# Third attention branch of a two-block network: upper turned pieces moved to idle score banks, a head pair's first scores put inside a projection, sum and gate of the output reordered

## What is computed

```python
qc = partial_rope(cq.reshape(B, S, C_HEADS, C_HEAD_DIM), positions)
kc = partial_rope(ck.reshape(B, S, C_HEADS, C_HEAD_DIM), positions)
for window, dil in ((128, 1), (512, 4), (2048, 16)):
    o_p, lse_p = dilated_window_attention(qc, kc, vc, window, dil)
wts = softmax(stack(lses), axis=0)
oc = sum(wts * stack(outs), axis=0)
yc = oc.reshape(B, S, C_WIDTH) * silu(cz)
```

## Time and profile before

| | |
|---|---|
| median of 3 runs | 3854.07 us (3852.71 to 3858.39) |
| the profiled execution | 3863.39 us, span 3861.7 us |
| TensorE busy | 3637.6 us, 94% of the span |
| VectorE, ScalarE, GpSimd busy | 1884.9, 1352.8, 1089.7 us |
| mean granted TensorE clock | 0.968 |

### The profile page before, as it was taken

One profiled execution on the slowest core, in us unless ns is written; L12 is line 12 of the kernel. 1 busy time (PEld: TensorE's weight loads), 2 busy tenths in 40 slices (PEclk: granted clock), 3 DMA queues, 4 the chain that ended last, 5 costly groups with the idle time before them and its releaser, 6 DMA issues.

```text
span 3861.7 us, 49543 instructions
## 1 busy us (share of the span) xinstructions
PE 3637.6 (94%) x19870; PEld 3212.0 (83%) x19870; DVE 1884.9 (49%) x3582; ACT 1352.8 (35%) x2965; POOL 1089.7 (28%) x794
## 2 busy tenths in 40 slices
PE   6999998988898999999999888899999999999998
PEld 5888887877777788888877777778999999999998
DVE  5444555455556364155635554555424546434543
ACT  3112444054443121044422444522225641224541
POOL 3633222311212345323323111223531013531102
PEclk9999999999999999999999999999999999999999
DMA  3121111411113311201122111152110013211012
GB/s 111 39 85 60 34 42 52 147 38 37 36 33 136 126 60 55 82 31 41 44 97 94 43 40 33 44 181 85 59 53 29 24 48 105 69 48 36 25 38 94
DMA packets 85478, 244.83 MB, mean 63 GB/s; under 512 B 10752, under 2 KB 24832, under 8 KB 85248
## 3 DMA queue, kind: packets, MB, share of 16 engines
q1 hardware_dynamic: 85248, 241.66, 18.8%
HBM read 191.09 MB, written 50.53 MB: 63 GB/s over the span
## 4 chain that ended last, share of the span: by engine, by line
PE 74%; DVE 12%; ACT 7%; issue 3%; POOL 2%; DMA 1%; SPq 0%; DVEq 0%; POOLq 0%; ACTq 0%
PE pj L1567 30%; PE pS L1567 26%; PE po L1817 3%; PE pS L1797 3%; PE pS L1799 2%; PE pS L1661 1%; PE pS L1662 1%; DVE tmp L2497 1%; DVE PC L2670 1%; ACT P L2029 1%; DVE tmp L2494 1%; DVE KK L2506 1%; PE po L1683 1%; PE po L1709 1%; ACT P L2022 1%
## 5 line engine op out<-in xcount | busy, mean ns | idle before, releaser
L2988 POOL TENSOR_SCALAR Whi<-stage 128x1024 fp32r<-128x1024 f32 (+3 forms) x252 | 259.6, 1030 | 1945.9 <-PE pj L1567 1241.7
L1567 PE MATMUL pj<-Hhi,Whi 128*128 128x512 f32 x1640 | 671.0, 409 | 51.4 <-DVE PC L2670 40.9
L1567 PE MATMUL pj<-Hlo,Whi 128*128 128x512 f32 x1640 | 654.7, 399 | 0.0
L1567 PE MATMUL pj<-Hhi,Wlo 128*128 128x512 f32 x1640 | 654.5, 399 | 0.0
L2990 POOL TENSOR_TENSOR Wlo<-stage,Whi 128x1024 fp32r<-128x1024 f32 (+3 forms) x252 | 599.5, 2379 | 21.0
L1567 PEld LDWEIGHTS pj<-Hhi,Whi 128*128 128x128 f32 x1640 | 320.3, 195 | 127.8 <-DVE PC L2670 48.8
L1567 PEld LDWEIGHTS pj<-Hhi,Wlo 128*128 128x128 f32 x1640 | 317.1, 193 | 70.2
L1567 PEld LDWEIGHTS pj<-Hlo,Whi 128*128 128x128 f32 x1640 | 318.8, 194 | 62.3
L1567 PE MATMUL pS<-Hhi,Whi 128*128 128x512 f32 x792 | 315.1, 398 | 20.9 <-DVE Hlo L2359 9.9
L1567 PE MATMUL pS<-Hlo,Whi 128*128 128x512 f32 x792 | 312.4, 394 | 0.0
L1567 PE MATMUL pS<-Hhi,Wlo 128*128 128x512 f32 x792 | 312.1, 394 | 0.0
(11 more groups left out here) (484 smaller groups left out, 7973.6 us busy)
## 6 DMA issues: line engine op xcount, KB each, us to landing
stage<-wstream SPq DMA_DIRECT2D x228, 512.0 KB, 3.6
merged<-Mb SPq DMA_DIRECT2D x32, 512.0 KB, 2.9
Mb<-merged SPq DMA_DIRECT2D x32, 512.0 KB, 5.2
gates<-tmp SPq DMA_DIRECT2D x48, 256.0 KB, 2.2
TH<-gates SPq DMA_DIRECT2D x24, 512.0 KB, 6.1
xres<-X SPq DMA_DIRECT2D x16, 520.0 KB, 2.9
xr<-xres SPq DMA_DIRECT2D x16, 520.0 KB, 3.9
X<-xT SPq DMA_DIRECT2D x16, 256.0 KB, 7.0
```

Of the source, the lines that this page charges most:

```text
L1567: x = pe.e.matmul(ps, w[a][:, v.koff + k * P:v.koff + k * P + P], moving(v.of, b, k, v.t0, v.n), start=k == 0 and i == 0, stop=k == v.K - ...
L2988: pool.e.tensor_scalar(upper, stage, 1.0, 0.0, ALU.mult, ALU.add).then_inc(*pool.tick("whi", c))
```

## The change

Three edits, all in the third branch of the first block:

1. In the last query block of a head (`i` = 3), the third and the fourth piece are turned into banks 3 and 5, which that step's own scores have left and the next scores (`i` = 0) don't need. Before, the fourth went to bank 3, and the third took one of the projection banks 0 and 1.
2. The first scores of the next head pair are issued inside the second half of the query projection, behind its fifth slice, instead of behind the whole of it; that projection moves from before `soft(s + 1)` into the list of projections behind it. So VectorE and ScalarE take the softmax of these scores before they rotate that projection.
3. `gather(s - 1)` stands behind the pieces of step `s`, not ahead of them. Its multiplication by the gate moves into `gather_out`, behind `soft(s + 1)`, as one operation on 64x512 for every two steps instead of two on 64x256.

```diff
--- before.py
+++ after.py
@@ -754,10 +754,10 @@
 
         def attended(soft, scores):
             self.banks = WIDE
-            turned = self.bank_free[3]
+            turned = self.bank_free[3], self.bank_free[5]
             self.bank_free[2:6] = [("masked", soft.id, m) for m in (0, 0, 1, 1)]
             if not diff:
-                self.bank_free[3] = turned
+                self.bank_free[3], self.bank_free[5] = turned
             self.mask_free = ("masked", soft.id, 1)
             self.th_free = self.phase()
             self.mb_free = ("scores", scores.id, 1)
@@ -896,11 +896,12 @@
             return dict(l=l, diff=False, s=s, j=j, h=h, qb=2 * i, nb=2 * i + 2, maps=[(h, 2 * i), (h, 2 * i + 1)],
                         col=96 + 12 * (s % 8), p=[0, 1])
 
-        def scores(s):
+        def scores(s, within=False):
             j, h, i = steps[s]
             keys = [qk["q"][i // 2], qk["k"][0]] + ([qk["k"][1]] if i >= 2 else [])
-            scored[s] = self.put("scores", **geometry(s), ready=[x for y in keys for x in y] + [cleared],
+            scored[s] = self.put("scores", **geometry(s), within=within, ready=[x for y in keys for x in y] + [cleared],
                                  free=[("masked", softened[s - 1].id, m) if s else None for m in (0, 0, 1, 1)])
+            return scored[s]
 
         def soft(s):
             softened[s] = self.put("soft_c", **geometry(s), scores=scored[s].id, p_free=p_free[:], masks=("masks_in", 2 * l + 1))
@@ -917,10 +918,10 @@
             u = self.put("turns_c", **geometry(s), **more, parts=parts, soft=softened[s].id,
                          pt_free2=("valued", valued[s - 1].id) if s else None)
             last = ("pt_low", s, l) + parts[-1][0:2]
-            if n == 3:
-
-                u["bank"], u["free"] = 3, ("masked", softened[s].id, 0)
-                self.bank_free[3] = last
+            if n > 1 and steps[s][2] == 3:
+
+                u["bank"], u["free"] = 2 * n - 1, ("masked", softened[s].id, n - 2)
+                self.bank_free[u.bank] = last
             elif n:
                 u["bank"], u["free"] = self.take()
                 self.bank_free[u.bank] = last
@@ -938,8 +939,7 @@
 
         def gather(s):
             j, h, i = steps[s]
-            u = self.put("gather", **geometry(s), i=i, valued=valued[s].id, y_free=self.y_free, z_ready=ztok[i // 2],
-                         tmp_free=self.tmp_free[3])
+            u = self.put("gather", **geometry(s), i=i, valued=valued[s].id, tmp_free=self.tmp_free[3])
             self.po_free = ("gathered", u.id)
             if i % 2:
                 gathered[s] = u
@@ -947,7 +947,7 @@
         def gather_out(s):
             j, h, i = steps[s]
             if s in gathered:
-                u = self.put("gather_out", **geometry(s), i=i, of=gathered[s], y_free=self.y_free)
+                u = self.put("gather_out", **geometry(s), i=i, of=gathered[s], z_ready=ztok[i // 2], y_free=self.y_free)
                 self.tmp_free[3] = ("lo", u.id)
                 if h:
                     self.ytok[i // 2].append(("lo", u.id))
@@ -968,15 +968,17 @@
                     amid[6], amid[7] = [q[0], g[3], k[0]], k[1:2]
                     fresh, turned = v[0:3], v[3:]
             todo = amid[s % 8]
+            for f in range(len(pieces(s))):
+                turn(s, f)
             if s:
                 gather(s - 1)
-            for f in range(len(pieces(s))):
-                turn(s, f)
             if s % 8 == 7 and j < 3:
 
-                self.run(q[1:2])
+                q[1]["inside"] = {4: [scores(s + 1, True)]}
+                todo = q[1:2] + todo
+            elif more:
+                scores(s + 1)
             if more:
-                scores(s + 1)
                 soft(s + 1)
             if s % 8 == 6 and j < 3:
                 read += [("scores", scored[s + 1].id, m) for m in range(2)]
@@ -2070,7 +2072,7 @@
 
     def gather_out(u):
         r = ROWS[u.h]
-        act.wait_ge(("y_out", u.of.id))
+        act.wait_ge(("y_out", u.id))
         for x in u.y_free:
             act.wait_ge(x)
         hi(m.Y[0][r, u.j, 512 * (u.i // 2):512 * (u.i // 2) + 512], m.tmp[3][r, :], u.id)
@@ -2672,18 +2674,18 @@
 
     def gather(u):
 
-        r, c, t0 = ROWS[u.h], 256 * (u.i % 2), 256 * u.i
+        r, c = ROWS[u.h], 256 * (u.i % 2)
         yt = m.tmp[3][r, c:c + 256]
         dve.wait_ge(("crossed", u.id))
-        dve.wait_ge(u.z_ready)
         phase_met(u)
         TT(yt, m.po[r, 0:256], yt, ALU.add).then_inc(*dve.tick("gathered", u.id))
-        dve.wait_ge(("gathered", u.id))
-        STT(out=yt, in0=yt, scalar=0.5, in1=m.Z[r, u.j, t0:t0 + 256], op0=ALU.mult, op1=ALU.mult).then_inc(
-            *dve.tick("y_out", u.id))
 
     def gather_out(u):
         r, t = ROWS[u.h], slice(512 * (u.i // 2), 512 * (u.i // 2) + 512)
+        dve.wait_ge(("gathered", u.of.id))
+        dve.wait_ge(u.z_ready)
+        STT(out=m.tmp[3][r, :], in0=m.tmp[3][r, :], scalar=0.5, in1=m.Z[r, u.j, t], op0=ALU.mult, op1=ALU.mult).then_inc(
+            *dve.tick("y_out", u.id))
         dve.wait_ge(("hi", u.id))
         for x in u.y_free:
             dve.wait_ge(x)
```

## The result

The changed kernel takes **3769.48 us** (median of 4 runs, 3763.28 to 3772.45), beside 3853.39 for the kernel before (4 runs, 3851.57 to 3858.39): a ratio of 0.9778, interval 0.9761 to 0.9795, 83.9 us less. The forecast was 3773, within 3747 to 3802. Its profiled execution took 3772.45 us (span 3770.7), 90.9 less than that of before.

The account below looks back on a forecast made before the run. TensorE, busy 94% of the span, bounds the kernel; only its idle time and slow clock can be won. Gains of 11.0 + 4.2 + 4.3 + 60.7 + 0.6 = 80.8 us from the 3854.07 median give 3773 us, range 3747 to 3802.

Parts of the forecast that it names:

- Steps 2 and 3: Third branch, projections' waits for banks: 1.38 us gained in step 2 and 0.52 in step 3, 8 times each.
- Steps 4 and 5: Third branch, value product and next transposes: only the weighing's 0.54 us counts, 8 times, 4.3 us; clock behind unchanged.
- The rival in which the clock holds: Step 5: the half-clock stretch behind step 4's value product also goes, 21.6 us more, giving 3752; chance 0.17.
- Step 7: Second query projection through next step 0: waits of 4.30 and 1.61 us and slow clock go, 10.1 us, 6 times, 60.7.
- the 1.61: TensorE's 1.61 us wait for the weighing at the next step 0, behind the query projection; forecast to go.
- the second rival: Step 7: the wait moves into the query projection as keys come late, 28 us given back, giving 3801; chance 0.12.
- the fourth: Rival: step 7's bank wait returns at the second key projection, so nothing lasting is won; about 3854, chance 0.03.
- The branch's end: Last value product of each third branch: its 2.7 us wait falls by 0.3, twice; bounds 0 and 2.7.
- The gate at nothing: Gate in its new place: 64 operations of 0.42 us become 32 of about 0.7, covered, costed at nothing.
- The rest: Queues, weights and banks elsewhere: 0 us change, with 3 us either way.
- my 4.2: Slow clock forecast to go around step 7: 2.6 us in query projection, 1.2 in value projections, 0.4 in transposes and scores.
- my third rival: The sum behind the pieces frees `po` up to 2.8 us later; uncovered in 54 steps, 151 us, giving 3924; chance 0.03.

Follow-up runs that it names:

- the gate moved alone: Kernel before with the gate moved into gather_out as one operation of 512, the sum left ahead of the pieces; 3818.1 us, ratio 0.9902.
- edit 3 alone: Kernel before with only the gather changed (sum behind the pieces, gate of 512 in gather_out); 3825.06 us, ratio 0.9922.
- the change without edit 1: Changed kernel with the bank edit undone, third piece in a projection bank again; 3788.64 us, ratio 0.984 to the kernel before.
- the change with the sum first: Changed kernel with the sum ahead of the pieces again, gate of 512 kept in gather_out; 3763.8 us, ratio 0.9768 to the kernel before.

## Why the prediction was right, step by step

The sum was 80.8 us, the profile gave 90.9, the medians 83.9. In the order of the steps, measured between the same value products in both profiles and summed over all pairs:

- **Steps 2 and 3**: forecast 1.90, measured 2.47, 8 times. Both waits went whole, as said. The projections behind them are also about 0.27 us shorter each (5.75 to 5.48): the first matmul after an idle time took 0.50 us instead of 0.39 and doesn't overlap one before it, and I didn't price that. 4.5 us more than forecast.
- **Steps 4 and 5**: forecast 0.54, measured 1.34 in the mean, 8 times. The value product waits for the sum (0.80), as said, and both waits together became 0.76 us shorter. The rest is the clock: "I take the clock behind it as unchanged" failed, since it stands at 0.62 over 4.5 us instead of 0.50. In the first pair of each branch the clock was about as high before as now, and only 0.78 and 0.95 us were won there. 6.4 us more than forecast, about 4.7 of them the clock's. The rival in which the clock holds fell for the change, where all eight pairs slow down. It holds in all pairs with a projection in step 4, and with the gate moved alone in two of eight.
- **Step 7**: forecast 10.1, measured 9.4 in the mean (8.9 to 9.8), 6 times. In the third pair of the first branch it is 9.65. Of these, 9.30 lie ahead of the next value projection (forecast 8.9): the 4.30, the 1.61 and the slow clock went, and the scores did not wait for their keys, so the second rival fell, and no wait moved to the second key projection, so the fourth did. Behind it, 1.4 us of clock come back (forecast 1.2), but the new 1.27 us ahead of the turned values takes 1.02 of it away. 4.0 us less than forecast. The term that I had missed is what follows once VectorE's work of step 7 is pushed together: ScalarE is late by it.
- **The branch's end**: forecast 0.3 each, measured 0.1 and 2.1. The last wait fell from 2.70 to 2.33 and from 2.99 to 2.33; in the second branch the clock behind it also stayed at 1.00, where it was 0.66 before. 1.6 us more than forecast.
- **The gate at nothing**: right; 0.68 us each (0.42 for the narrow one), behind work of ScalarE.
- **The rest**: forecast 0, measured 1.2 outside the branches, within the scatter of what lies there.

19.7, 10.7, 56.7 and 2.2 make 89.3 of the 89.7 us.

The waits were forecast well. That the median came within 4 us of the forecast is in part luck: two terms were some 11 us too small and the largest was 4 too large, and the profiled execution of the kernel before lay some 9 us above its median, that of the changed kernel 3 above its own, so 90.9 us in the profiles are 83.9 in the medians.

**The parts overlap.** Alone the three edits take 113 us from the branches, together 89.7; taken out of the change one at a time, they are worth 26.2, 16.6 and 25.8. About 20 of the 23 us of difference lie in step 7 and the step 0 behind it: edit 3 alone takes 0.92 off a wait that edit 1 removes anyway; the slow clock behind the 1.61 (1.6 of my 4.2) goes with edit 2, and in three of six pairs with edit 1 too; and the 1.02 us of new wait come only where edits 1 and 2 meet. These three are 16 us; the others are differences of the clock that I can't assign.

**What was wrong in the reasons.** I counted the sum's place behind the lower halves as part of the gain in steps 2, 4 and 5. It was all the gate's. The sum behind frees `po` later, the mechanism of my third rival, but only where no projection lies between: 4 to 7 us in all, and not 151.

**What stays open.** Why the clock falls behind one wait and not behind an equal one, even in the same kernel. What the edits won by the clock is therefore measured and not explained. I made no kernel that changes only what precedes a wait.

## What to carry to other kernels

Where VectorE feeds the engine that bounds the kernel, look first at who shares its time with GpSimd: moving the one SBUF-only operation (here a gate) out from ahead of work that TensorE waits for was worth more than reordering around it. Put a projection between the pieces and the product that needs them in every step, also in the last pair, before shaving fractions off the wait itself. And when gains at one place are added up, check that each removes another wait: here a fifth of the single gains was counted twice.

## What the runs showed of the hardware

The granted clock doesn't follow from the length of the wait ahead. Over the 8 us behind a wait of 3.38 us it was 0.62 to 0.79 in five of six pairs with edit 3 alone and 1.00 in one, and 1.00 in four of six pairs of the change without edit 1 and 0.81 or 0.82 in two. Over the 4.5 us behind waits of 0.62 and 1.70 us in a row it was 0.62 in all eight pairs of the change with the sum first, and with the gate moved alone 0.62 to 0.70 in six pairs and 1.00 in two. The Trainium skill ("TensorE: Matmul & The Clock Gate", HAM oscillation) warns of single idle gaps longer than 0.62 and 1.70 us; by that rule no slow stretch would follow these two, and the rows don't agree.

A VectorE operation whose operands all lie in SBUF took 2.60 us beside a GpSimd split of 2.39, and 0.68 without; two others together took 4.26 instead of 1.4 beside one of 2.71. The Trainium skill ("SBUF — State Buffer", two separate sides) has VectorE and GpSimd lock a shared pair of ports, and these rows agree.

A projection behind an idle time cost about 0.27 us more at full clock than one that followed other work (5.75 against 5.48).
